# Layer norm centred by the mean of seven tiles with an exact correction, and the second output projection interleaved with the end of the recurrence

## What is computed

```python
u = depthwise_conv(u) + b_dw
mu = jnp.mean(uf, axis=-1, keepdims=True)
var = jnp.mean(jnp.square(uf - mu), axis=-1, keepdims=True)
u = ((uf - mu) * lax.rsqrt(var + EPS) * ln_g + ln_b)
return jax.nn.silu(u) @ w_pw2 + b_pw2
```

```python
hg = hgrn2_readout(o_lf + flip(o_lb), p[..., O_HG:O_FN], hg_norm_g[l])   # rms norm per head, gain, silu gate
y = jnp.concatenate([attn, hg, fn], axis=-1) @ w_out[l]                  # 512 + 256 + 256 columns
x_new = x + g1 * y
```

## Time and profile before

| what | us |
|---|---|
| median of three runs | 1067.35 |
| the profiled execution: device time | 1068.82 |
| the profiled execution: span from first to last instruction | 1066.9 |
| PE busy in the span | 1026.4 (96%) |
| DVE busy | 656.0 (61%) |
| ACT busy | 510.7 (48%) |
| mean granted clock of PE | 0.994 of full |

### The profile page before, as it was taken

How to read it: one execution, slowest core, us unless ns; L and a number is a source line. 1 busy time by engine, 2 the same in 40 slices (tenths; PEclk the granted TensorE clock), 3 DMA queues, 4 the chain that set the end, 5 groups by cost and what they waited for, 6 DMA issues and landing times.

```text
span 1066.9 us, 16529 instructions
## 1 busy us (share of the span) xinstructions
PE 1026.4 (96%) x7104; PEld 888.4 (83%) x7112; DVE 656.0 (61%) x720; ACT 510.7 (48%) x585; POOL 70.6 (7%) x84
## 2 busy tenths in 40 slices
PE   7999989999999999999999999999998899999997
PEld 5996778888989886988989897898557778888886
DVE  5566567676768664767877545352579664454444
ACT  6467555344345324753444444554466554434434
POOL 0000200000000000000000000000237000000000
PEclk9999999999999999999999999999999999999999
DMA  7542447667564874458787555222000345555441
GB/s 265 203 159 79 158 168 264 227 232 250 203 235 156 279 217 155 150 186 292 256 300 282 198 190 230 80 95 104 0 1 2 123 147 205 185 172 195 178 177 40
DMA packets 34046, 187.69 MB, mean 176 GB/s; under 512 B 3776, under 2 KB 8128, under 8 KB 15296
## 3 DMA queue, kind: packets, MB, share of 16 engines
q1 hardware_dynamic: 25920, 155.66, 41.5%
q0 software_dynamic: 7200, 27.27, 7.4%
q10 hardware_dynamic: 864, 3.88, 1.0%
HBM read 181.09 MB, written 1.05 MB: 171 GB/s over the span
## 4 chain that ended last, share of the span: by engine, by line
PE 87%; DVE 5%; ACT 4%; DMA 2%; issue 1%; POOL 0%; SPq 0%; DVEq 0%; ACTq 0%
PE PS L269 12%; PE PS L271 12%; PE PS L270 12%; PE PS L581 11%; PE PS L583 11%; PE PS L582 11%; PE PS L1067 2%; PE PS L614 1%; DMA raw<-wstream 1%; PE PS L318 1%; PE PS L320 1%; PE PS L319 1%; PE PS L1289 1%; DVE w_lo L256 1%; PE PS L477 1%
## 5 line engine op out<-in xcount | busy, mean ns | idle before, releaser
L256 DVE TENSOR_TENSOR w_lo<-raw,w_hi 128x2048 fp32r<-128x2048 f32 x140 | 320.5, 2292 | 210.6 <-ACT w_hi L252 210.3
L252 ACT ACTIVATE w_hi<-raw 128x2048 fp32r<-128x2048 f32 x141 | 268.9, 1910 | 180.6 <-PE PS L271 92.2
L581 PE MATMUL PS<-w_hi,a_hi 128*128 128x512 f32 x512 | 203.2, 397 | 1.5 <-DVE w_lo L256 1.5
L582 PE MATMUL PS<-w_lo,a_hi 128*128 128x512 f32 x512 | 199.8, 390 | 0.0
L583 PE MATMUL PS<-w_hi,a_lo 128*128 128x512 f32 x512 | 199.8, 390 | 0.0
L269 PE MATMUL PS<-a_hi,w_hi 128*128 128x256 f32 (+1 forms) x576 | 174.0, 302 | 3.3 <-DVE a_lo L538 2.1
L270 PE MATMUL PS<-a_lo,w_hi 128*128 128x256 f32 (+1 forms) x576 | 170.4, 296 | 0.0
L271 PE MATMUL PS<-a_hi,w_lo 128*128 128x256 f32 (+1 forms) x576 | 170.3, 296 | 0.0
L269 PE MATMUL PS<-h_hi,w_hi 128*128 128x256 f32 x528 | 149.7, 283 | 0.4 <-DVE h_lo L767 0.4
L271 PE MATMUL PS<-h_hi,w_lo 128*128 128x256 f32 x528 | 149.4, 283 | 0.0
L270 PE MATMUL PS<-h_lo,w_hi 128*128 128x256 f32 x528 | 149.4, 283 | 0.0
(11 more groups left out here) (318 smaller groups left out, 1150.9 us busy)
## 6 DMA issues: line engine op xcount, KB each, us to landing
raw<-wstream SPq DMA_DIRECT2D x142, 1024.0 KB, 4.8
modraw<-wmod POOLq DMA_DIRECT2D x48, 512.0 KB, 4.9
U<-CU SPq DMA_DIRECT2D x32, 142.0 KB, 4.3
cst<-cst ACTq DMA_DIRECT2D x1, 1632.0 KB, 10.5
mlw<-mlw ACTq DMA_DIRECT2D x1, 1280.0 KB, 5.7
X<-xT SPq DMA_DIRECT2D x2, 512.0 KB, 5.2
CROW<-crow POOLq DMA_DIRECT2D x1, 1024.0 KB, 5.3
CTX<-ctxT POOLq DMA_DIRECT2D x1, 1024.0 KB, 8.6
```

Of the source, the lines that this page charges most:

```text
L252: nc.scalar.activation(w_hi[:, slot, :], raw[:, rslot, :], ACT.Copy).then_inc(S("hi_done"), 1)
L256: dve.tensor_tensor(w_lo[:, slot, :], raw[:, rslot, :], w_hi[:, slot, :].bitcast(F32), ALU.subtract).then_inc(S("lo_done"), 1)
L581: nc.tensor.matmul(out, a_hi[:, k, src, ts], wh, start=k == 0, stop=False, skip_group_check=True)
L582: nc.tensor.matmul(out, a_hi[:, k, src, ts], wl, start=False, stop=False, skip_group_check=True)
```

## The change

In the layer norm, PE sums tiles 0 to 6 only, before the convolution of tile 7; `MU` is the mean of those seven, and DVE and ACT centre and square the seven tiles while PE convolves the last. Tile 7 is then centred by the same mean. With d the centred values, the sum of d over all features is that of tile 7 alone, so one product with ones on tile 7 gives their mean m, and the variance is the mean of d*d less m*m, exactly. DVE forms m*m and the variance and subtracts m from all eight tiles (`without`). `ctx_sums` moves behind the sums of squares, `ctx_factor` into the norm of the following block (ACT, after its squares), and 14 idle products become 4.

In the third layer, `MIX` is split into buffers of its own (`o_hi`, `o_lo`), tiles 6 and 7 before tiles 4 and 5. The first unit of the projection is written out on PE: six tiles x two halves x three products are placed between and after the recurrence's last products, and tiles 4 and 5 follow. ACT squares straight from PSUM and DVE gates straight from PSUM, so the copy `OH` goes; ACT makes the high part of the second unit before `hg_o`, and DVE makes the low part of the first unit before its last two merges and that of the second unit in two halves. Tiles 4 and 5 are scaled and rounded one by one.

The diff, cut, unchanged lines left out or marked "..." and indentation reduced:

```diff
@@ -231,9 +231,15 @@
+o_hi = at("o_hi", 193.5, KT * T, F32R)[:, :].rearrange("p (k t) -> p k t", k=KT)
+o_lo = [at(f"o_lo{r}", kib, 4 * T, F32R)[:, :].rearrange("p (k t) -> p k t", k=4)
+        for r, kib in enumerate((201.5, 182))]
...
+def by_chunk(ap, c):
+    return ap.rearrange("p (m c v) -> p m c v", c=2, v=CHUNK)[:, :, c, :]
...
@@ -278,7 +284,7 @@
...
@@ -287,7 +293,8 @@
-            last = split_mm(outs[nb], H, L, a_hi[:, k, src, :], a_lo[:, k, src, :], k == 0, k == KT - 1)
+            xh, xl = (o_hi[:, k, :], o_lo[k // 4][:, k % 4, :]) if mixed else (a_hi[:, k, src, :], a_lo[:, k, src, :])
+            last = split_mm(outs[nb], H, L, xh, xl, k == 0, k == KT - 1)
...
@@ -441,6 +448,8 @@
+    if n == 3:
+        ctx_factor(act)
     norm_factor(act, n, after)
...
@@ -525,18 +534,26 @@
+MIX_ORDER = ((0, 1, 2, 3), (0, 1, 3, 2))
...
+def mix_operands(m, ks):
+    if m:
+        r = ks.start // 4
+        return o_hi[:, ks, :], o_lo[r][:, ks.start - 4 * r:ks.stop - 4 * r, :]
+    return a_hi[:, ks, MIX_HALF[0], :], a_lo[:, ks, MIX_HALF[0], :]
...
+        ks = slice(2 * j, 2 * j + 2)
...
-        nc.scalar.activation(a_hi[:, 2 * j:2 * j + 2, MIX_HALF[m], :], MIX[:, 2 * j:2 * j + 2, :], ACT.Copy)\
-            .then_inc(S("mix_hi"), 1)
+        nc.scalar.activation(mix_operands(m, ks)[0], MIX[:, ks, :], ACT.Copy).then_inc(S("mix_hi"), 1)
...
-        eng.wait_ge(S("mix_hi"), 4 * m + j + 1)
-        eng.tensor_tensor(a_lo[:, ks, MIX_HALF[m], :], MIX[:, ks, :],
-                          a_hi[:, ks, MIX_HALF[m], :].bitcast(F32), ALU.subtract).then_inc(S("act_lo"), 1)
+        hi_part, lo_part = mix_operands(m, ks)
+        eng.wait_ge(S("mix_hi"), 4 * m + MIX_ORDER[m].index(j) + 1)
+        eng.tensor_tensor(lo_part, MIX[:, ks, :], hi_part.bitcast(F32), ALU.subtract).then_inc(S("act_lo"), 1)
...
@@ -1081,18 +1098,25 @@
 conv(6)
-for k in range(KT):
-    if k == 5:
-        conv(7)
+for k in range(KT - 1):
...
-    i = nc.tensor.matmul(PS[:, 6, 0:T], ones, HN[:, k, :], start=k == 0, stop=k == KT - 1)
+    i = nc.tensor.matmul(PS[:, 6, 0:T], ones, HN[:, k, :], start=k == 0, stop=k == KT - 2)
 i.then_inc(S("ln_sum"), 1)
+conv(7)
...
+def squares(k):
+    pe.wait_ge(S("ln_sq"), (1, 1, 2, 2, 3, 3, 4, 5)[k])
+    return nc.tensor.matmul(PS[:, 6, T:2 * T], ones, SQ[:, k, :], start=k == 0, stop=k == KT - 1)
...
+for k in range(4):
+    squares(k)
+pe.wait_ge(S("ln_d"), 5)
+nc.tensor.matmul(PS[:, 5, 0:T], ones, HN[:, 7, :], start=True, stop=True).then_inc(S("ln_sum"), 1)
+for k in range(4, KT):
+    i = squares(k)
+i.then_inc(S("ln_ss"), 1)
 ctx_sums(pe)
-for k in range(KT):
-    pe.wait_ge(S("ln_sq"), k // 2 + 1)
-    i = nc.tensor.matmul(PS[:, 6, T:2 * T], ones, SQ[:, k, :], start=k == 0, stop=k == KT - 1)
-i.then_inc(S("ln_ss"), 1)
-idle_products(0, 14)
+idle_products(0, 4)
...
@@ -1330,8 +1354,30 @@
+out2 = [PS[:, 4, nb * T:(nb + 1) * T] for nb in range(2)]
+early, late = (0, 1, 2, 3, 6, 7), (4, 5)
...
+def out2_high(nb, ks, start=False):
+    for k in ks:
+        nc.tensor.matmul(out2[nb], wblk(U_OUT2 % SLOTS, nb * KT + k)[0], o_hi[:, k, :],
+                         start=start and k == 0, stop=False, skip_group_check=True)
...
+def out2_low_weights(nb, ks):
+    for k in ks:
+        nc.tensor.matmul(out2[nb], wblk(U_OUT2 % SLOTS, nb * KT + k)[1], o_hi[:, k, :],
+                         start=False, stop=False, skip_group_check=True)
...
+def out2_low_inputs(nb, ks):
+    for k in ks:
+        i = nc.tensor.matmul(out2[nb], wblk(U_OUT2 % SLOTS, nb * KT + k)[0], o_lo[k // 4][:, k % 4, :],
+                             start=False, stop=k == 5, skip_group_check=True)
+    return i
...
 hg_level(1, 4)
 hg_level(1, 5)
+pe.wait_ge(S("hi_done"), U_OUT2 + 1)
+pe.wait_ge(S("mix_hi"), 7)
+out2_high(0, early, True)
 pe.wait_ge(S("hg_copied"), 13)
...
@@ -1340,9 +1386,33 @@
 i.then_inc(S("hg_o"), 1)
+out2_high(1, early)
 pe.wait_ge(S("hg_osq"), 1)
 nc.tensor.matmul(PS[:, 0, :], blk, SQO, start=True, stop=True).then_inc(S("hg_oss"), 1)
-out_units_pe(pe, U_OUT2, "o2", 4, sums=5)
+pe.wait_ge(S("lo_done"), U_OUT2 + 1)
+out2_low_weights(0, early)
+out2_low_weights(1, early)
+pe.wait_ge(S("act_lo"), ACT_LO["o2"] + 3)
+out2_low_inputs(0, early)
+out2_low_inputs(1, early)
+pe.wait_ge(S("mix_hi"), 8)
+for nb in range(2):
+    out2_high(nb, late)
+    out2_low_weights(nb, late)
+pe.wait_ge(S("act_lo"), ACT_LO["o2"] + 4)
+out2_low_inputs(0, late)
+out2_low_inputs(1, late).then_inc(S("unit_done"), 1)
+for j in range(1, N_OUT):
+    if j == 1:
+        pe.wait_ge(S("out2_half"), 1)
+    else:
+        pe.wait_ge(S("lo_done"), U_OUT2 + j + 1)
+    if j >= 2:
+        pe.wait_ge(S("x_updated"), 4 * 4 + j - 1)
+    feature_unit((U_OUT2 + j) % SLOTS, [PS[:, 4 + j % 2, nb * T:(nb + 1) * T] for nb in range(2)], 0,
+                 middle=(lambda: pe.wait_ge(S("lo_done"), U_OUT2 + 2)) if j == 1 else None, mixed=True)\
+        .then_inc(S("unit_done"), 1)
+norm_pe(pe, 5)
...
@@ -1515,19 +1585,26 @@
-for k in range(5, KT):
-    conv_read(k)
+conv_read(5)
+conv_read(6)
 table(LN_EXP)
 act.wait_ge(S("ln_sum"), 1)
-nc.scalar.activation(MU, PS[:, 6, 0:T], ACT.Copy, scale=1.0 / D).then_inc(S("ln_a"), 1)
+nc.scalar.activation(MU, PS[:, 6, 0:T], ACT.Copy, scale=1.0 / (7 * P)).then_inc(S("ln_a"), 1)
...
+def centred_squares(j):
+    ks = slice(2 * j, min(2 * j + 2, 7)) if j < 4 else slice(7, 8)
+    act.wait_ge(S("ln_d"), j + 1)
+    nc.scalar.activation(SQ[:, ks, :], HN[:, ks, :], ACT.Square).then_inc(S("ln_sq"), 1)
...
 for j in range(4):
-    act.wait_ge(S("ln_d"), j + 1)
-    nc.scalar.activation(SQ[:, 2 * j:2 * j + 2, :], HN[:, 2 * j:2 * j + 2, :], ACT.Square)\
-        .then_inc(S("ln_sq"), 1)
-ctx_factor(act)
-act.wait_ge(S("ln_ss"), 1)
-nc.scalar.activation(RS, PS[:, 6, T:2 * T], ACT.Ln, scale=1.0 / D, bias=prm_eps).then_inc(S("ln_a"), 1)
-act.wait_ge(S("ln_a"), 2)
+    centred_squares(j)
+conv_read(7)
+centred_squares(4)
+act.wait_ge(S("ln_sum"), 2)
+nc.scalar.activation(MU, PS[:, 5, 0:T], ACT.Copy, scale=1.0 / D).then_inc(S("ln_a"), 1)
+act.wait_ge(S("ln_d"), 9)
+nc.scalar.activation(RS, RS, ACT.Ln, bias=prm_eps).then_inc(S("ln_a"), 1)
+act.wait_ge(S("ln_a"), 3)
...
 table(SILU)
 for j in range(4):
...
@@ -1717,31 +1794,32 @@
 hg_pair_decay(1, 3)
 hi(act, U_OUT2)
-hg_pair_decay(1, 4)
-hg_pair_decay(1, 5)
...
-        act.wait_ge(S("hg_sc"), 13)
-    if j == 2:
-        act.wait_ge(S("hg_out"), 1)
-mix_split_act(act, 1, mix2_ready, (0, 1))
+    if j == 3:
+        act.wait_ge(S("fn_read"), 3)
...
+mix_split_act(act, 1, mix2_ready, (0, 1, 3))
+hg_pair_decay(1, 4)
+hg_pair_decay(1, 5)
+act.wait_ge(S("hg_sc"), 12)
+hi(act, U_OUT2 + 1)
 act.wait_ge(S("hg_o"), 1)
...
-    by_chunk = lambda ap: ap.rearrange("p (m c v) -> p m c v", c=2, v=CHUNK)[:, :, c, :]
-    i = nc.scalar.activation(by_chunk(OH), by_chunk(PS[:, 2 + c, :]), ACT.Copy)
-i.then_inc(S("hg_r"), 1)
-act.wait_ge(S("hg_r"), 1)
-nc.scalar.activation(SQO, OH, ACT.Square).then_inc(S("hg_osq"), 1)
+    i = nc.scalar.activation(by_chunk(SQO, c), by_chunk(PS[:, 2 + c, :], c), ACT.Square)
+i.then_inc(S("hg_osq"), 1)
 act.wait_ge(S("hg_oss"), 1)
...
-act.wait_ge(S("hg_r"), 2)
+act.wait_ge(S("hg_r"), 1)
...
-mix_split_act(act, 1, mix2_ready, (2, 3))
-hi(act, U_OUT2 + 1)
+for k in (4, 5):
+    act.wait_ge(S("hg_out"), k - 3)
+    i = nc.scalar.activation(o_hi[:, k, :], MIX[:, k, :], ACT.Copy)
+i.then_inc(S("mix_hi"), 1)
 hi(act, U_OUT2 + 2)
...
@@ -1965,13 +2043,28 @@
+def without(ks):
+    dve.tensor_tensor(HN[:, ks, :], HN[:, ks, :], MU.unsqueeze(1).to_broadcast([P, ks.stop - ks.start, T]),
+                      ALU.subtract).then_inc(S("ln_d"), 1)
...
+dve.wait_ge(S("cv_read"), 7)
+dve.wait_ge(S("ln_a"), 1)
+for ks in (slice(0, 2), slice(2, 4), slice(4, 6), slice(6, 7)):
+    without(ks)
...
-dve.wait_ge(S("ln_a"), 1)
-for j in range(4):
-    ks = slice(2 * j, 2 * j + 2)
-    dve.tensor_tensor(HN[:, ks, :], HN[:, ks, :], MU.unsqueeze(1).to_broadcast([P, 2, T]), ALU.subtract)\
-        .then_inc(S("ln_d"), 1)
-dve.wait_ge(S("ln_a"), 3)
+without(slice(7, 8))
+dve.wait_ge(S("ln_a"), 2)
+dve.tensor_tensor(RS, MU, MU, ALU.mult).then_inc(S("ln_d"), 1)
+dve.wait_ge(S("ln_sq"), 5)
+without(slice(0, 2))
+without(slice(2, 4))
+dve.wait_ge(S("ln_ss"), 1)
+dve.wait_ge(S("ln_d"), 6)
+dve.scalar_tensor_tensor(RS, PS[:, 6, T:2 * T], 1.0 / D, RS, ALU.mult, ALU.subtract).then_inc(S("ln_d"), 1)
+without(slice(4, 6))
+without(slice(6, 8))
+dve.wait_ge(S("ln_d"), 11)
+dve.wait_ge(S("ln_a"), 4)
...
@@ -2209,20 +2302,35 @@
 pair_queries(1, 5)
+lo(dve, U_OUT2)
 pair_copy(1, 4)
 pair_copy(1, 5)
-lo(dve, U_OUT2)
 mix_split_lo(dve, 1, (0, 1))
-dve.wait_ge(S("hg_r"), 1)
+dve.wait_ge(S("hg_osq"), 1)
...
-dve.wait_ge(S("hg_osq"), 1)
-dve.tensor_tensor(OH, OH, XO[:, 6:8, :].rearrange("p k t -> p (k t)"), ALU.mult).then_inc(S("hg_g"), 1)
-dve.wait_ge(S("hg_r"), 3)
+for c in range(2):
+    i = dve.tensor_tensor(by_chunk(OH, c), by_chunk(PS[:, 2 + c, :], c),
```

(22 more changed lines are left out.)

## The result

| | median us | runs from to | ratio to before, 95% |
|---|---|---|---|
| before, same session | 1066.95 | 1065.71 to 1068.12 | |
| the changed kernel | 1059.03 | 1058.71 to 1060.49 | 0.9925 (0.9912 to 0.9938) |

The changed kernel is faster by 0.75%, 7.9 us. The forecast was 1059.0. The profiled execution took 1059.16 (span 1057.3), 9.6 us of span under that of before. The next views say where the 9.6 lie.

The account below looks back on a forecast made before the run. PE carries 87% of the chain, so the prediction sought PE's waits and work that need not stand there. Layer norm 3.6 plus recurrence 4.7 gave 8.3 us, from 1067.35 to a median of 1059.0, range 1057.3 to 1061.7.

Parts of the forecast that it names:

- Layer norm, 3.6: Layer norm: 20 fewer PE sum instructions between convolution 7 and the finished squares; Ln starts 3.6 us earlier (3.0 to 3.85).
- hand-over of 0.3: Layer norm, DVE's variance: late bound of 420.3 if each of two hand-overs took 0.3 us more; 419.7 expected.
- End of the recurrence, 4.7: Recurrence's end into second output projection: first unit 5.7 us earlier, but the weights' load and split chain limits the gain to 4.7.
- the change of tile form: Recurrence, six products placed in PE's 0.83 us wait: a change of tile form may add some tenths; 0.2 us taken.
- The 1.5 for the stretch of half clock: First projection unit on PE: 16 products at the 1.2 GHz level after the wait; removing that saves 1.5 us.
- the bound of 6.0: Projection's weight chain: if both loads took 6.0 us, the stretch's longest, the recurrence gain would be 2.6 us.
- The weights do not bind: Rival, end of the projection: last low part waits less than counted; gain 9.4 us, time 1057.9; chance 0.14.
- Half does not do what it says: Rival, layer norm: tile 7's centring and correction late on DVE, first high part no earlier; gain 4.7, 1062.6; chance 0.06.
- Slower by the clock in `pw2`: Rival, start of `pw2`: PE's clock falls because 14 idle products became 4; 1069.5 us; chance 0.03.
- A further term: Rival: 6.0 us loads, a new half-clock stretch, or six products missing their gap; gain 6 to 7, 1060.9; chance 0.22.

Follow-up runs that it names:

- both moves of the chain: Changed kernel with the sixth weight unit's low part behind the last add: 1058.99 us; with the second unit's second low half ahead of tiles 4 and 5's: 1059.15 us.
- the zero products in the kernel before: Kernel before with eight products on zeros in PE's 2.13 us wait for tiles 4 and 5: 1066.8 us against 1067.55, ratio 0.9991.
- the half alone: Kernel before with only the layer norm's edits: 1063.15 us, ratio 0.9964; where 28.09 is given, with only the recurrence's edits: 1062.25 us, ratio 0.9952.
- the better version: Changed kernel with first and second unit products moved into PE's waits and the sixth unit's low part behind the last add: 1056.95 us, again 1057.84.

## Why the prediction was right

*Layer norm, 3.6: right, and by its own steps.* The squares end 7.7 us after the start of convolution 7, as summed. The variance, of which no row existed, was bounded from both sides; Ln starts 8.47 us after convolution 7, where the sum gave 8.5 (419.7 less 411.22). So no hand-over of 0.3 was added. The sum of seven tiles cost nothing, the last two subtractions were hidden by the table load, and the first `pw2` product came after a wait of 0.39, forecast 0.4.

*End of the recurrence, 4.7: right in mechanism, 0.4 too small in the trace.* First unit 7.0 us after the `SC` product, as its last part forecast (the 839.2 of its sum would be 7.2). Weights bind and PE is done first, as forecast; both ends of that chain were tested. Three terms were off by tenths. The second unit's low part was done 7.1 us after the `SC` product (834.56), not 7.4, of which 0.2 is the change of tile form: from the start of the last-but-one merge to the `SC` product it is 1.75 us (1.71 before), so it costs nothing. The chain took 18.0 us, not 18.3. Add to Ln took 2.75, not 2.6; the rows of before already had 864.96 - 862.20 = 2.76, and with it the prediction's own chain gives a gain of 4.5, not 4.7. The 1.5 for the stretch of half clock measured 1.5 on PE. Two slips moved nothing: three units from 839.2 end at 856.5, not 856.3, and the chain runs over the fourth and sixth units, not the third and fifth.

*Loads.* The two of the chain took 4.7 and 4.9 us; transfers of this stretch have a median of 4.8. The longest in the changed kernel took 5.5, so the bound of 6.0 was not reached. The Trainium skill's 6.15 us for 1 MB (DMA: Bandwidth & Descriptors, Bandwidth), which stands there for transfers that GpSimd issues, is not what this trace shows either.

*The point itself was partly luck.* 8.3 was forecast, the traces gave 8.7, the medians 7.9 against the kernel before of the same session and 8.3 against the 1067.35 of the forecast. An error of half a microsecond in either half would have been invisible in the medians.

*Rivals.* "The weights do not bind" is refuted by the missing idle time before the add, by both moves of the chain, and by the zero products in the kernel before, of whose 1.5 us only 1.3 arrive. "Half does not do what it says" is refuted by the half alone. "Slower by the clock in `pw2`" did not happen, even without the idle products. A further term did not show.

*What the argument lacked.* It priced the half clock behind the wait of 2.13 us, but passed over the same thing 13 us earlier: 64 products with the states in 3.29 us in the trace of before, behind a wait of 2.37, where 2.08 is their time at full clock. That cost stands in both kernels, so the forecast did not suffer; the better version takes it.

## What to carry to other kernels

Where an engine is busy but its work is not needed there, count how many of its instructions stand between an event and the one that the chain follows; that number times the row's pitch was right to a tenth. Before taking such work away, ask whether it kept PE busy across a wait: moved alone, it gained nothing. Price such a loss on the engine itself: 1.5 us of PE's time read as 1.3 at the end of the stage, because something else bound there. And after filling the waits of the bound engine, look for the chain beside it (here load, high part, low part, and the queue in which the low part stands): it decides how much of the gain arrives.

## What the runs showed of the hardware

- The clock, in the 14 traces, leaving out the first 20 and the last 10 us of each: each of the 16 waits of PE of 1.99 to 2.47 us has a stretch at the 1.2 GHz level that begins within 1.1 us of its end, in three places (before the states, before tiles 4 and 5, before the squares with the sums moved). The waits of 0.39 to 1.25 us shown here have none. In between the wait alone does not decide it: in code that no edit touches, a stretch stands behind the wait of 1.62 us near 103 us in 3 of the 14 traces, behind one of 1.2 to 1.5 us near 147 us in 3, behind one of 1.48 us near 771 us in 4, and behind one of 1.70 us near 744 us in none. In three places one stretch cost PE 1.5 to 1.8 us: 3.76 against 2.26 us for 18 products of 128x256, 3.57 against 2.08 for the 64 with the states, 5.41 against 3.62 for 16 squares. Useful or zero products in the wait removed it each time that it was tried. The Trainium skill (TensorE: Matmul & The Clock Gate, HAM oscillation) tells of long waits for data; here short waits inside a tuned kernel did it.
- One kernel's executions differ in such stretches where its code is the same (100 to 110, 145 to 155, 770 to 780 us): up to 3.2 us between two profiles that no edit explains. Intervals measured from a common event inside the trace repeated far better. The layer norm was 11.67 or 11.68 wherever it was the changed one. The changed recurrence was 27.86, 27.77, 27.85 and 27.91 in the kernels that hold the whole change and none of the moves of its chain, and 28.09 in the half alone, whose two loads took 0.1 us longer each than in the changed kernel's first trace. This is why the tenths above can be read at all; a difference of two or three of them proves little.
